# Dividing product 5 of the input projection's channel groups, with VectorE's, ScalarE's and GpSimd's work laid out anew

## The reference

```python
def reference(x, norm_g, w_in, conv_w, conv_b, w_a_out, w_b_out, w_o, final_g):
    for layer in range(DEPTH):
        h = rmsnorm(x, norm_g[layer])
        proj = h @ w_in[layer]
        b_a, c_a, x_a, z_a, q, k, v, z_b, g_a, g_b = jnp.split(proj, split_points, axis=-1)
        y_a = short_conv_branch(b_a, c_a, x_a, z_a, ...)     # silu(z) * B * conv3(C * x) @ w_out
        y_b = retention_branch(q, k, v, z_b, w_b_out[layer]) # rotary(q), rotary(k), decay, silu(z)
        merged = jax.nn.sigmoid(g_a) * y_a + jax.nn.sigmoid(g_b) * y_b
        x = x + merged @ w_o[layer]
    return rmsnorm(x, final_g)
```

## Time and profile before

| | us |
|---|---|
| median of 3 runs | 1364.84 (1364.6 to 1365.53) |
| the profiled execution | 1365.87 |
| its span | 1364.1 |
| TensorE busy | 1351.8 |
| VectorE, ScalarE, GpSimd busy | 1060.0, 608.3, 413.7 |

### The profile page before, as it was taken

One profiled execution on the slowest core, in us unless ns is written; L12 is line 12 of the kernel. 1 busy time (PEld: TensorE's weight loads), 2 busy tenths in 40 slices (PEclk: granted clock), 3 DMA queues, 4 the chain that ended last, 5 costly groups with the idle time before them and its releaser, 6 DMA issues.

```text
span 1364.1 us, 17294 instructions
## 1 busy us (share of the span) xinstructions
PE 1351.8 (99%) x6642; PEld 1142.7 (84%) x6642; DVE 1060.0 (78%) x1097; ACT 608.3 (45%) x821; POOL 413.7 (30%) x381
## 2 busy tenths in 40 slices
PE   9999999999999999999999999999999999999997
PEld 7788888888888888888888888888888888888886
DVE  6898465677878777678888778748776998788887
ACT  6843233433333333333333433438778433433445
POOL 0100112344444554444443444315444001100002
PEclk9999999999999999999999999999999999999999
DMA  9646445344433433476666666757768699945443
GB/s 333 216 132 214 141 110 166 95 108 109 109 101 86 108 93 99 136 183 172 176 162 166 147 166 179 223 201 252 267 223 267 141 332 308 235 158 201 162 85 124
DMA packets 112979, 234.81 MB, mean 172 GB/s; under 512 B 7680, under 2 KB 50816, under 8 KB 108032
## 3 DMA queue, kind: packets, MB, share of 16 engines
q1 hardware_dynamic: 104112, 194.87, 42.2%
q0 software_dynamic: 8640, 38.80, 16.0%
q10 hardware_dynamic: 144, 0.02, 0.0%
HBM read 169.70 MB, written 55.57 MB: 165 GB/s over the span
## 4 chain that ended last, share of the span: by engine, by line
PE 92%; ACT 2%; issue 1%; DVE 1%; DMA 1%; POOL 1%; SPq 1%; POOLq 0%; ACTq 0%; DVEq 0%
PE psum L2625 15%; PE psum L2627 15%; PE psum L2628 15%; PE psum L2768 7%; PE psum L2766 7%; PE psum L2767 7%; PE psum L2549 3%; PE psum L2551 3%; PE psum L2550 3%; PE psum L2538 3%; PE psum L2540 3%; PE psum L2541 3%; PE psum L2670 2%; PE psum L2672 2%; PE psum L2671 2%
## 5 line engine op out<-in xcount | busy, mean ns | idle before, releaser
L1146 ACT ACTIVATE slots<-work 128x1024 fp32r<-128x1024 f32 (+1 forms) x166 | 169.5, 1027 | 418.0 <-PE psum L2628 292.1
L2625 PE MATMUL psum<-hc,slots 128*128 128x512 f32 x912 | 355.0, 389 | 0.0
L2627 PE MATMUL psum<-hc,slots 128*128 128x512 f32 x912 | 354.9, 389 | 0.0
L2628 PE MATMUL psum<-hc,slots 128*128 128x512 f32 x912 | 354.8, 389 | 0.0
L2628 PEld LDWEIGHTS psum<-hc,slots 128*128 128x128 f32 x912 | 171.2, 188 | 35.8
L2625 PEld LDWEIGHTS psum<-hc,slots 128*128 128x128 f32 x912 | 171.2, 188 | 35.3 <-issue 0.4
L2627 PEld LDWEIGHTS psum<-hc,slots 128*128 128x128 f32 x912 | 171.2, 188 | 34.8
L1435 ACT ACTIVATE last_slot<-arena 128x1024 fp32r<-128x1024 f32 x112 | 118.6, 1062 | 163.0 <-PE psum L2768 157.3
L2766 PE MATMUL psum<-last_slot 128*128 128x512 f32 (+1 forms) x452 | 175.3, 388 | 0.0
L2768 PE MATMUL psum<-last_slot 128*128 128x512 f32 (+1 forms) x452 | 175.0, 387 | 0.0
L2767 PE MATMUL psum<-last_slot 128*128 128x512 f32 (+1 forms) x452 | 175.0, 387 | 0.0
(11 more groups left out here) (228 smaller groups left out, 2496.1 us busy)
## 6 DMA issues: line engine op xcount, KB each, us to landing
work<-w_channel SPq DMA_DIRECT2D x80, 512.0 KB, 4.0
work<-w_channel POOLq DMA_DIRECT2D x40, 512.0 KB, 5.5
arena<-w_last SPq DMA_DIRECT2D x19, 1024.0 KB, 7.9
qk<-qk_scratch SPq DMA_DIRECT2D x32, 512.0 KB, 3.4
arena<-w_last POOLq DMA_DIRECT2D x9, 1024.0 KB, 10.5
v_raw<-value_scratch SPq DMA_DIRECT2D x32, 256.0 KB, 3.9
arena<-gate_scratch SPq DMA_DIRECT2D x16, 512.0 KB, 6.8
value_c<-w_value SPq DMA_DIRECT2D x10, 512.0 KB, 4.8
```

Source lines behind the costliest of these rows:

```text
L1146: nc.scalar.activation(slots[:, u % SLOTS, 0, 0:columns_of(u)], src, ACT.Copy, scale=-1.0 if negated(u) else 1.0).then_inc(w_hi, 1)
L2625: nc.tensor.matmul(bank, slot[:, 0, w], x_high, start=product in STARTS and j == 0, stop=False, skip_group_check=True)
L2627: nc.tensor.matmul(bank, slot[:, 0, w], x_low, start=False, stop=False, skip_group_check=True)
L2628: last = nc.tensor.matmul(bank, slot[:, 1, w], x_high, start=False, stop=j == 3, skip_group_check=True)
```

## The change

Product 5 is divided in groups 2 to 17 (`FIFTHS`), its halves one behind the other. Its T1, T2 and T4 have no area of their own: both sets are stored to DRAM once (group 1), and SP loads `hx` twice a group, for product 5 when the group before has ended product 4, for product 4 when product 5's second half has ended. GpSimd makes four more `second_sums`, for product 5. `s1` becomes an accumulating DMA on GpSimd's queue into e, which SP now loads first (one more load of 0.5 MB a group); s1 and s3 stand behind all `second_sums`. ScalarE applies SiLU as one function, in place; GpSimd's products for it, one of its gate products and VectorE's early gate product are gone. VectorE's order is new: in turn groups product 4's low part comes directly behind product 5's sum, then the two low parts of the first rotated half and the four remaining steps of the second half, then product 7's sum. The sets T of product 5 are made in group 0, those of product 4 a little later than before.

```diff
-              if (p != THIRD_HALF or g in THIRDS) and (p != LAST_HALF or g in TWICE)]
+FIFTHS = range(2, GROUPS - 2)
+LAST_HALF, THIRD_HALF, FIFTH_HALF = 7, 8, 9
+UNIT_TABLE = [(g, p) for g in range(GROUPS) for p in (0, 1, 2, 3, FIFTH_HALF, 4, 5, 6, LAST_HALF, THIRD_HALF)
+              if (p != THIRD_HALF or g in THIRDS) and (p != LAST_HALF or g in TWICE) and (p != FIFTH_HALF or g in FIFTHS)]
 UNITS = VALUE_UNITS + len(UNIT_TABLE)
...
-    return 3 * QUARTER if n in (5, 6) and halved_product(g, product_at(n)) else 2 * HALF
+    return 3 * QUARTER if n in (3, 5, 6) and halved_product(g, product_at(n)) else 2 * HALF
...
-    ROLES.append(dict(a=r["c"], b=r["b"], c=r["a"], d=r["e"], e=r["d"]))
+    ROLES.append(dict(a=r["c"], b=r["b"], c=r["a"], d=r["d"], e=r["e"]))
...
-        return hx[:, ("T1", "T2", "T4").index(name), part] if product == 4 else third_parts[name][:, part]
+        return third_parts[name][:, part] if product == 3 else hx[:, ("T1", "T2", "T4").index(name), part]
...
-        return set_at(g + 1, 1 if g in THIRDS and product == 4 else 6)
+        return set_at(g + 1, 1 if product == 5 or g in THIRDS and product == 4 else 6)
...
+        def load_hx(product):
+            n = int(product == 5)
+            sp.dma_start(hx[:, 2].bitcast(F32), hx_d[n, :, 2]).then_inc(t4_in, 16)
+            sp.dma_start(hx[:, 0:2].bitcast(F32), hx_d[n, :, 0:2]).then_inc(t1_t2_in, 16)
...
+            if g in FIFTHS:
+                sp.wait_ge(unit_done, ended_at(g - 1) + 1)
+                load_hx(5)
...
-                load_work(g + 1, "d", 3)
+                sp.wait_ge(w_ready, fifth_ended_at(g) + 1)
+                load_work(g + 1, "e", 3)
...
+                if g in FIFTHS:
+                    sp.wait_ge(unit_done, fifth_ended_at(g) + 1)
+                    load_hx(4)
+                if g in THIRDS:
+                    sp.wait_ge(w_ready, ended_at(g) + 1)
+                    load_work(g + 1, "d", 3)
...
         def s1(g):
-            a, b, c, d, e = buffers(g)
+
+            if g:
+                work_loaded(g, "e")
+                pool.dma_start(work[ROLES[g]["e"]][:, :], w_channel[g, 2], accum_op=ALU.add).then_inc(s1_in, 16)
+            else:
+                a, b, c, d, e = buffers(g)
+                work_loaded(g, "b")
+                work_loaded(g, "d")
+                pool.wait_ge(w_ready, unit_of(1, 3, 1) + 1)
+                nc.gpsimd.tensor_tensor(e, b, d, ALU.add).then_inc(summed, 1)
+
+        def s3(g):
...
         def s2(g):
             a, b, c, d, e = buffers(g)
+            if g:
+                pool.wait_ge(s1_in, 16 * g)
             pool.wait_ge(w_ready, unit_at(g, 1) + 1)
             nc.gpsimd.tensor_tensor(a, e, a, ALU.add).then_inc(summed, 1)
...
-            w = work[ROLES[g]["d" if product == 4 else "a"]]
+            w = work[ROLES[g][{3: "a", 4: "d", 5: "e"}[product]]]
...
-        def silu(g, j):
-            i, m = g - QZS.start, g % 2
-            z = (tp_c11, tp_v2, tp_first, tp_v)[j][m][:, 1, :]
-            pool.wait_ge(silu_sig_made, 4 * i + j + 1)
-            nc.gpsimd.tensor_tensor(z, z, silu_sig[:, :], ALU.mult).then_inc(silu_made, 1)
...
         for g in range(GROUPS):
-            turn, turned = kind_of(g) == "turn", g > 0 and kind_of(g - 1) == "turn"
             conv = g > 0 and kind_of(g - 1) == "conv"
             if conv:
                 conv_gate(g - 1, 1)
-                conv_gate(g - 1, 0)
+            if g in FIFTHS:
+                second_sums(g, 5)
+            if conv:
                 conv_gate(g - 1, 2)
-            if turned:
-                silu(g - 1, 2)
-            if turned:
-                silu(g - 1, 3)
             if g in THIRDS:
+                second_sums(g, 4)
                 second_sums(g, 3)
-            if g in TWICE:
+            elif g in TWICE:
                 second_sums(g, 4)
-            if turn:
-                silu(g, 0)
             if g + 1 < GROUPS:
                 s1(g + 1)
...
-            nc.scalar.activation(silu_sig[:, :], z, ACT.Sigmoid).then_inc(silu_sig_made, 1)
+            after(g, (None, 7, 3, 4)[j])
+            z = (None, tp_v2, tp_first, tp_v)[j][g % 2][:, 1, :]
+            nc.scalar.activation(z, z, ACT.Silu).then_inc(silu_made, 1)
...
+                    if n == 6 and g in FIFTHS and g not in THIRDS:
+                        low(u + 1)
+                elif n == 3 and halved_product(g, 5):
+                    second_first(g, 5)
+                elif n == FIFTH_HALF:
+                    second_rest(g, 5, range(1))
+                    if g in THIRDS:
+                        low(u + 2)
+                    second_rest(g, 5, range(1, 3))
+                    add(g, 5)
+                    if g not in THIRDS:
+                        low(u + 2)
...
-                    for step in {0: (0,), 2: (1, 2, 3, 4, 5)}.get(p, ()):
+                    for step in ({0: (0,), 1: (1, 2, 3, 4), 2: (5,)} if g in FIFTHS else {0: (0,), 2: (1, 2, 3, 4, 5)}).get(p, ()):
                         turn(last, 0, step)
-                    if p == 3:
+                    if p == (4 if g in FIFTHS else 3):
                         turned(last, 0)
-                    for step in {3: (0, 1, 2, 3), 4: (4, 5)}.get(p, ()):
+                    for step in ({2: (0, 1), 4: (2, 3, 4, 5)} if g in FIFTHS else {3: (0, 1, 2, 3), 4: (4, 5)}).get(p, ()):
                         turn(last, 1, step)
-                    if p == 4:
+                    if p == (5 if g in FIFTHS else 4):
...
+                    if product == 5:
+                        second_half(g, 5)
```

More of the change, by code:

```diff
@@ L1022, in _ @@
                 s2(g + 1)
-            if turn:
-                silu(g, 1)
             if g + 1 < GROUPS:
@@ L2110, in _ @@
                 if place_of(u)[1] == LAST_HALF:
+                    low(u + 1)
+                    low(u + 2)
+            elif u >= VALUE_UNITS and place_of(u)[0] in FIFTHS and place_of(u)[1] in (0, 1, 2, 3, 4, 6, FIFTH_HALF):
+                conv = place_of(u)[0] - 1 in CONVS
+                if place_of(u)[1] == 0 or place_of(u)[1] in (1, 2) and not conv:
+                    low(u + 2)
+                if place_of(u)[1] == 0 and conv:
+                    low(u + 3)
+                if place_of(u)[1] == FIFTH_HALF:
                     low(u + 1)
```

220 lines of the change are left out of this document (134 added, 86 removed).

## The result

The changed kernel takes 1381.79 us (median of 4, 1379.81 to 1383.32) where the kernel before took 1365.04: 1.0122 times as long, 95% interval 1.0109 to 1.0134, 16.8 us more. The forecast was 1363.9 with a range to 1373.5. The profiled execution is the fastest of the four, 1379.81 us, 13.9 more than that of before.

What follows compares the result with a forecast made beforehand. TensorE, busy 1351.8 of 1364.1 us, was taken as the bound. Profiled 1365.9 - 0.4 (conv groups) - 0.5 (turn groups) = 1365.0, or 1363.9 us for the median; range 1357.2 to 1373.5.

Steps and rivals of the forecast that it cites:

- Part 2: Conv groups: loop through GpSimd of 37.35 us against TensorE's 36.67; 3.7 of 4.1 us gained is lost, net -0.4.
- the landing: Conv groups: time L for s1's accumulating DMA to land before s2 can start, taken as 6.0 us.
- Part 3: Turn groups: VectorE's work ahead of sum 7 makes product 4's first half wait 0.45 us; net -0.5 us.
- Part 1: TensorE's matmuls: each divided product 5 saves 0.51 us, 8.2 us over 16 groups; set-up in group 0 costs nothing.
- the constant: Conv groups: the loop without s1's landing, 29.65 us plus 1.7 for slow VectorE and GpSimd pairs, 31.35.
- the lag that is free: Conv groups: the loop may lag 2.6 us before TensorE first waits, at product 3's second half.
- the worst row: Turn groups: all four sums at 0.54 us extra, a wait of 1.25, group 38.33 us, +5.9.
- Part 4: SiLU in one operation, table loads, hx and work loads put at nothing; hx in time with 1 us to spare in conv groups.
- C: Rival: s1's landing delays s2 and what hangs on it; 1369.5 us at L = 6.7, 1376 with Part 3's worst; chance 0.20.
- D: Rival: full blocking of VectorE by GpSimd's sums in turn groups, 3.0 us each group, 1376 us at the least; chance 0.05.

Runs made afterwards that it cites:

- hx_first: Changed kernel with s1's DMA ahead of product 4's and 3's sums, four rotation steps behind product 7's sum, conv groups' product 4 hx loads issued earlier: 1362.2 us.
- narrow_sums: Changed kernel with GpSimd's four sums for product 4 in turn groups on 64 columns in place of 256 (output wrong): 1375.4 us.
- none_divided: Changed kernel with product 5 left whole in every group, all else kept: 1377.9 us.
- none_s1_early: Changed kernel with product 5 whole everywhere and s1's DMA issued ahead of product 4's and 3's sums: 1364.6 us.
- s1_early: Changed kernel with s1's DMA issued ahead of product 4's and 3's sums in all groups: 1376.6 us.

## Why the prediction was wrong, point by point

The forecast was a small gain, -0.4 us in the conv groups and -0.5 in the turn groups; the trace has +6.3 and +8.4. Two steps failed. In Part 2 the round's constant and the landing were taken too short and the free lag too long. In Part 3 the sum of product 7 was put 0.8 us too early.

- **What bounds the kernel, and Part 1 (the matmuls): right.** Halves of 2.13 and 2.80 us; conv groups of 36.69 in hx_first and turn groups of 37.09 in narrow_sums are the forecast 36.67 and 37.08. The set-up cost nothing in groups 0 and 1 (38.08 and 37.57, as before). Group 2 did not gain: it has a wait of 0.6 us ahead of product 3's first half and is 37.55 in hx_first, against 37.48 before.
- **Part 2, the landing: nearly right.** 6.0 taken, 6.2 measured as the median of those groups. The mean of the seven rounds is 6.25, and over seven rounds that is 1.8 us.
- **Part 2, the constant: 31.35 taken, 31.89 measured.** The 0.3 that came up to y was nearly made up by the low part; 0.5 came in the eight sums, one of which took 1.72 us in place of 0.74 (381.23 above), beside VectorE's low part (381.06). Over seven rounds that is 3.8 us. I had put one slow pair there.
- **Part 2, the lag that is free: 2.6 taken, 2.1 there.** I looked for the first wait at product 3's second half. It was at product 6: not its split, which had 3.1 us, but product 3's first addition behind the split on VectorE, 0.95 us later, for a bank. And the first conv group did not start from no lag: s1 was issued 31.8 us after its start where I had 29.7, so that the lag was 2.6 at once and nothing was absorbed. 3.8 for the constant, 1.8 for the landing and the 1.1 that wasn't absorbed make the 6.7 between -0.4 and +6.3.
- **Part 2, the view of the cause: wrong.** I took the loop as product 5's work. none_divided shows that s1's DMA behind all second sums closes a round even with product 5 whole. The comparison that was missing is simple: s1 was 2.4 us between two points of the chain and became 6 to 8, with 2.3 us of idle between s1 and s2 before.
- **Part 3: the mechanism right, the size wrong.** Not three but four slow pairs: 1.9 us, not 1.4. And product 3's low part stands ahead of product 5's additions, which start at 21.7, not 21.4. Sum 7 ends at 33.4, not 32.6; product 4's first half starts 1.4 late (the row's wait is 1.24 of it), not 0.45; the group is 38.57, close to the worst row's 38.33, which I had as the upper end. +8.4 in place of -0.5.
- **Part 4: right.** SiLU, the table loads and the loads of work cost nothing (none_s1_early), hx was in time in the changed kernel. But its cover was s1's lateness: in s1_early product 4's halves lost 12.2 us.
- **Rivals.** C named the place (s2 behind s1's landing), with too low a price, since it rested on the same constant. D's rule is taken up below. The range failed because it allowed the upper end of one part only: C at 6.7 together with Part 3's worst row was 1376, and I cut the range at 1373.5, though slow pairs lengthen the loop and the turn groups alike and are not independent.

## What to carry to other kernels

When a sum becomes a DMA, its price on the path is the landing and not the engine's time; ask first whether its inputs are there earlier, and issue it ahead of what it stood behind. Here one moved line was worth 13 us without the division, and 5 with it, until the hx loads were moved too. When a slack is to absorb a lag, look for all that the waiting instruction needs, banks too, and what stands in front of each on its engine. Place VectorE's operations with two SBUF inputs where GpSimd is idle, above all not beside its widest ones; and take the worst cases of terms with one cause together.

## What the runs showed of the hardware

Where a VectorE instruction with two SBUF inputs met a GpSimd sum in these traces, one held up the other. Beside 256-wide sums (0.74 us alone) VectorE's 0.69 us became 1.11 to 1.23, and GpSimd's sums 1.06 to 1.18, so the price was 0.4 to 0.5 us for each. From start to start they are 1.1 to 1.3 us apart, where VectorE's alone are 0.6 apart and GpSimd's 0.7, so that strict turns would make 1.3. Beside a 1024-wide sum it was 2.2 us for one operation (2.88 in place of 0.69), and that sum was itself 2.70 in place of 2.40. The Trainium skill ("SBUF — State Buffer", section "Who interferes with whom") says that the other engine "fully blocks (not throttle)". I had held 1.11 to 1.23 against it; the 2.88 us agree with it, and the smaller numbers are close to what it gives when both sides' instructions are short and alternate. GpSimd's sum of 1.72 us agrees too: it ended 0.6 us behind VectorE's low part of 1.29 us (381.06 + 1.29 = 382.35, 381.23 + 1.72 = 382.95). What was too high in rival D was its arithmetic, a whole sum for each pair, 3.0 us where 1.9 were measured.

In the changed kernel s1's accumulating DMA of 0.5 MB took 5.7 to 8.4 us to land. Removing 3 MB of hx traffic a group changed nothing in conv groups and took 0.7 us off the median in turn groups; moving the DMA right behind it shortened neither. What else lengthens it isn't shown.
